# Sums of squares by a rounded square and its rest: two single-pass matmuls in place of one in fp32

## The chip, the cores and the metric

The kernel runs on one core of a Trainium2 chip. The metric is the device time of one execution in microseconds (us). The engines are TensorE (PE in the profile; its weight loads are listed as PEld), VectorE (DVE), ScalarE (ACT), GpSimd (POOL) and SyncE (SP), which here only issues the loads of weights.

## What is computed

One step of a one-layer encoder for 256 prompt tokens, 16 meta tokens and 32 sample tokens. The normalised input is multiplied by `w_in`. From the product come an attention branch with 16 heads and an mLSTM branch with 4 heads, and their gated outputs are multiplied by `w_out`. The change touches three RMS norms of the attention branch: that of the query latent (1536 columns), that of the queries (per head 128 columns and a rotary part of 64), and that of the keys (per head 128 columns):

```python
def rmsnorm(x, g):
    xf = x.astype(jnp.float32)
    y = xf * lax.rsqrt(jnp.mean(xf * xf, axis=-1, keepdims=True) + EPS)
    return (y * g.astype(jnp.float32)).astype(x.dtype)

q = (rmsnorm(cq_raw, q_a_norm) @ w_q_up).reshape(B, T, MLA_HEADS, QK_NOPE + QK_ROPE)
q_nope = rmsnorm(q[..., :QK_NOPE], q_nope_norm)
q_pe = rope(rmsnorm(q[..., QK_NOPE:], q_rope_norm), pos)
kv = (ckv @ w_kv_up).reshape(B, S, MLA_HEADS, QK_NOPE + V_HEAD)
k_nope = rmsnorm(kv[..., :QK_NOPE], k_nope_norm)
s = einsum(q_nope, k_nope) + einsum(q_pe, k_pe); p = softmax(s * ATTN_SCALE); attn = einsum(p, v)
```

## The kernel before

Features lie on the 128 partitions and tokens along the free dimension: 288 queries, 432 keys. Every large product is made of *units*. A unit is a 128-row slice of a weight matrix in `raw`. ScalarE casts it to fp32r, a rounded 32-bit form that TensorE takes in one pass (`whi`, line 490), VectorE subtracts the cast from the original (`wlo`, line 857), and TensorE does three fp32r matmuls for each 128 columns (`mm3`, lines 1297, 1300, 1301). ScalarE and VectorE work three units ahead of TensorE (`AHEAD`), and can start on unit k+3 when TensorE is done with unit k-1, because there are four slots.

Each engine runs a program written out by hand in a fixed order. The function `steps` does the split of unit k+3 and then calls `hooks(k)`, in which the small work of a stage is put. So what an engine does in hook k is behind the split of unit k+3 and ahead of the split of unit k+4, and a wait in a hook holds back every later split. On TensorE the hook of unit k comes behind the matmuls of unit k.

Stages that matter here:

- **ckv group** (32 units of 512 columns, 12 matmuls each). After units 2 to 13 `cq_squares` sums the squares of the query latent over the partitions by a matmul with a matrix of ones, in fp32 (line 1363). GpSimd makes the squares (line 1800) into `sqb`, which has three slots.
- **Eight head pairs.** A pair has 12 units for the queries (`q_units`, 9 matmuls each) and 4 for keys and values (`kv_units`, 18 matmuls each). Pair n+1 is projected while the attention of pair n is done in the hooks: `k_squares` at hook 1 (line 1499), `scores` of the two heads at hooks 5 and 8 (line 1510), `transposes` at 9 and 12, `weighted` at 11 and 13, and `q_squares` for the next pair at hook 14 (line 1457; at hook 13 in the first pair). The attention of the last pair runs in the hooks of the first mLSTM group, whose units have 12 matmuls.
- **At the end of a pair**, VectorE copies the raw keys out of PSUM (`k_evict`, line 994), then makes two products for the rotary part (lines 985, 986) and scales the two query heads in place (line 989). GpSimd squares the keys (line 1830), adds the rotary products (line 1835) and scales them for two heads (line 1840, `qpm`). ScalarE makes the inverse roots of the queries (`q_rstd`, lines 581 and 583, at hook 15) and then copies the values out (`v_evict`, line 611), which frees PSUM banks 1 and 2 for the next pair's queries.
- **Early in the next pair**, ScalarE makes the inverse roots of the keys at hook 1 (`k_rstd`). It waits there until the queries are scaled (`q_fin`) and the rotary part is scaled (`qp_fin`), because the roots of keys and queries share one buffer, `rsb`. VectorE scales the keys at hooks 2 and 3 (`k_norm`, line 1013). `scores` of the first head waits for the first of them.

```python
def k_rstd(phase, i, j):
    for t in range(2):
        b = 6 + t
        if t == 0:
            act.wait_ge(q_fin, 2 * j + 2)
            act.wait_ge(qp_fin, 2 * j + 2)
        rstd(rs2[:, t, :], bank[b][:, 0:NKV], 1.0 / NOPE, b, use(phase, b, 0, i), k_rs)
```

Of the kernel before, what the change touches and what calls it, by code (L numbers as in the profile page):

```python
# [28 lines left out]
P = 128  # L29
# [138 lines left out]
def hymba_step(nc, x_prompt, x_sample, cache_ckv, cache_kpe, state_C, state_n, state_m, meta, norm_gain,  # L168
# [8 lines left out]
    with ctx:  # L177
# [13 lines left out]
        nraw = sb("nraw", [72, NT])  # L191
        epsc = sb("epsc", [P, 1])
        gate_b = sb("gate_b", [ML_HEADS, 3])
        attnT = sb("attnT", [P, MLA_HEADS, NQ])

        def c(name, rows=P):
            a, w = CONST_AT[name]
# [30 lines left out]
        qpm = [sb2(f"qpm{h}", [P, SEQ + WIDE]) for h in range(2)]  # L228
        kn = sb2("kn", [P, 2, NKX])
        vt = sb2("vt", [P, 4, 2 * V_HEAD])  # L230
        sqb = sb2("sqb", [P, 3 * NQ])
        rsb = sb2("rsb", [P, 3 * NQ])
        rope1 = sb2("rope1", [P, NT])
        rope2 = sb2("rope2", [P, NT])
        rotq = sb2("rotq", [P, P])
# [5 lines left out]
        prob = keep(pa)("prob", [P, PROB_COLS])  # L241
        probT = keep(pa)("probT", [P, 608])
        pa.close()
        ckvf = sb2("ckvf", [P, KC, NT])
        p2.close()
        cqraw = attnT
        sq3 = sqb[:, :].rearrange("p (t n) -> p t n", t=3)
        sq2 = sqb[:, :].rearrange("p (t n) -> p t n", t=2)
        rs3 = rsb[:, :].rearrange("p (t n) -> p t n", t=3)
# [86 lines left out]
        gsc_d = sem("scaled_gains")  # L336
# [136 lines left out]
        def _(act):  # L473
# [76 lines left out]

            def ckv_hooks(k):

                if k == 16:
                    act.wait_ge(full[4], use("ckv", 4) + 1)
                    nc.scalar.activation(rs3[:, 0, :], bank[4][:, 0:NQ], ACT.Ln, scale=1.0 / Q_LORA,
                                         bias=epsc[:, :]).then_inc(free[4], 1)
                    act.wait_ge(free[4], use("ckv", 4) + 1)
                    nc.scalar.activation(rs3[:, 0, :], rs3[:, 0, :], ACT.Exp, scale=-0.5).then_inc(cq_rs, 1)
                if 18 <= k < 18 + KQ:
                    t = k - 18  # L560
                    act.wait_ge(cq_n, t + 1)
                    nc.scalar.copy(cqhi[:, t, :], cqraw[:, t, :]).then_inc(cq_hi, 1)
# [36 lines left out]
            def q_rstd(phase, i, n):  # L599

                for t in range(3):
# [2 lines left out]
                    rstd(rs3[:, t, :], bank[b][:, 0:NQ], 1.0 / (NOPE if t < 2 else ROPE), b,  # L604
                         use(phase, b, nth, i), q_rs)

            def v_evict(phase, i, n):
# [6 lines left out]
            def latent(k):  # L614
                if k == 7:
# [12 lines left out]
            q_rstd("bulk0", 0, 0)  # L628
            act.wait_ge(ck_out, 32)
            act.wait_ge(ck_tail_out, 32)  # L630
            v_evict("bulk0", 0, 0)
# [30 lines left out]

            def attention(phase, i, j):
                def hooks(k):
                    if k == 1:
                        k_rstd(phase, i, j)
                    if k == 6:
                        exps(phase, i, j, 0)
                    if k == 10:
                        pt_main(phase, i, j, 0)  # L670
                        exps(phase, i, j, 1)
                    if k == 12:
                        attn_evict(phase, i, j, 0)
# [10 lines left out]
            act.wait_ge(prob_zero, 1)  # L684
            for j in range(0, 6):
                steps(PAIR_UNITS, pair_units(j + 1), pair_units(j + 2), attention("step", j, j))
                v_evict("step", j, j + 1)
            steps(PAIR_UNITS, pair_units(7), big_units(U_ML, T_ML, 0, 2), attention("step", 6, 6))
            v_evict("step", 6, 7)


# [157 lines left out]
        def _(dve):  # L849
# [53 lines left out]
            ts_(rope1[:, 0:P], rot, G[:, G_KR:G_KR + 1], None, ALU.mult).then_inc(gsc_d, 1)  # L903

            def ckv_hooks(k):
                if 17 <= k < 17 + KQ + 1:
# [72 lines left out]
            def q_norm(phase, i, n):  # L979

                nth = 0 if phase == "bulk0" else 3
                if phase == "bulk0":
                    dve.wait_ge(kp_out, 64)
                dve.wait_ge(full[7], use(phase, 7, nth, i) + 1)
                tt(rope2[:, 0:NQ], bank[7][:, 0:NQ], sinT[:, N_META:NT], ALU.mult).then_inc(free[7], 1)
                stt(rope1[:, 0:NQ], qp[:, :], gsc[:, 1:2], cosT[:, N_META:NT], ALU.mult, ALU.mult).then_inc(qp_c, 1)
                for t in range(2):
                    dve.wait_ge(q_rs, 3 * n + t + 1)
                    stt(qn[:, t, :], qn[:, t, :], gsc[:, 0:1], rs3[:, t, :], ALU.mult, ALU.mult).then_inc(q_fin, 1)
# [5 lines left out]

            def first_pair(k):
                latent(k)
                if k == KQ - 1:
                    q_evict("bulk0", 0, 0)
                    dve.wait_ge(full[6], use("latent", 6, 2) + 1)  # L1000
# [3 lines left out]
            for t in range(2):  # L1004
                k_evict("bulk0", 0, 0, t)
            q_norm("bulk0", 0, 0)

            def k_norm(j, t):
                dve.wait_ge(k_rs, 2 * j + t + 1)
# [26 lines left out]

            def attention(phase, i, j):
                def hooks(k):
                    if k in (2, 3):
                        k_norm(j, k - 2)  # L1040
                    if k == 5:
                        maxima(phase, i, j, 0)
                    if k == 7:
# [6 lines left out]
                    if k == KQ - 1 and phase == "step":  # L1050
                        q_evict(phase, i, j + 1)
                    if k == 12:
                        pt_minor(phase, i, j, 1)
                return hooks

            def pair_end(i, n):
                for t in range(2):
                    k_evict("step", i, n, t)
                q_norm("step", i, n)

            def big_units(u):
                return lambda k: unit(u + k, k)
# [229 lines left out]
        def _(pe):  # L1292
# [64 lines left out]
            def cq_squares(k):  # L1357
                if 2 <= k < 2 + KQ:
                    t = k - 2
                    if t == 0:  # L1360
                        fill("ckv", 4)
                    pe.wait_ge(cq_sq, t + 1)
# [87 lines left out]
            def q_squares(phase, i, n):  # L1450

                first = phase == "bulk0"
                for t in range(3):
                    b = 4 + t
                    pe.wait_ge(q_sq, 3 * n + t + 1)
# [38 lines left out]
            def k_squares(phase, i, j):  # L1494
                for t in range(2):
                    b = 6 + t
                    pe.wait_ge(k_sq, 2 * j + t + 1)
# [488 lines left out]
```

## Time and profile before

| | |
|---|---|
| median of 3 runs | 2138.77 us (2137.19 to 2139.71) |
| the profiled execution | 2138.62 us |
| its span in the profile | 2137.0 us |
| mean granted TensorE clock | 0.997 |
| busy share: PE, DVE, ACT, POOL | 98%, 49%, 42%, 10% |

The profile is one execution. The span is the time from its first to its last instruction; 1.6 us of the execution lie around it. A share of busy time is a mean over stages. Lines such as L1499 are lines of the kernel before. A matmul with fp32 operands leaves two records for one instruction, and the records of matmuls overlap: what one costs is read from start to start, not from its duration. Starts and durations in a timeline are in us.

### The profile page before, as it was taken

How to read it: one execution, taken by the hardware profiler on the slowest of the kernel's cores; microseconds unless marked ns; L12 is line 12 of the kernel's file. 1: busy time of each engine (PE TensorE's matmuls, PEld its weight loads, DVE VectorE, ACT ScalarE, POOL GpSimd, SP SyncE). 2: the span in 40 equal slices, each digit the busy share in tenths (PEclk: the TensorE clock that was granted, in tenths of full speed). 3: DMA queues.
4: the chain of work that ended last, by engine and by line, in shares of the span. 5: the costliest groups of instructions: out<-in, count | busy, mean ns of one | idle time of the engine just before them, and what ended most of it. 6: DMA issues, size and time to landing. Idle time of an engine off the chain costs nothing.

```text
span 2137.0 us, 38018 instructions
## 1 busy us (share of the span) xinstructions
PE 2089.4 (98%) x15062; PEld 2029.1 (95%) x15062; DVE 1047.2 (49%) x1868; ACT 891.4 (42%) x1751; POOL 218.5 (10%) x292
## 2 busy tenths in 40 slices
PE   4999999999999999999999999999999999999997
PEld 3999999999999899998999999999999999999997
DVE  4544565655544444443444444444445654444443
ACT  4543454545443333343333444444444543333332
POOL 1000123333200000000000000000001100000000
PEclk9999999999999999999999999999999999999999
DMA  7555433232455454554545555555555555555553
GB/s 195 155 164 159 117 121 94 89 104 80 119 149 163 119 163 122 153 145 118 178 123 155 167 167 164 165 167 167 165 163 166 164 181 183 180 180 183 186 188 105
DMA packets 189984, 321.92 MB, mean 151 GB/s; under 512 B 20524, under 2 KB 65680, under 8 KB 189424
## 3 DMA queue, kind: packets, MB, share of 16 engines
q1 hardware_dynamic: 182464, 296.92, 47.0%
q0 software_dynamic: 5488, 15.11, 2.1%
q10 hardware_dynamic: 1872, 7.60, 1.4%
q8 instruction: 119, 1.95, 0.4%
q14 instruction: 41, 0.34, 0.1%
HBM read 309.96 MB, written 9.62 MB: 150 GB/s over the span
## 4 chain that ended last, share of the span: by engine, by line
PE 97%; DMA 1%; DVE 0%; ACT 0%; issue 0%; ACTq 0%; POOL 0%; POOLq 0%; DVEq 0%; SPq 0%
PE bank L1297 29%; PE bank L1301 28%; PE bank L1300 28%; DMA xt<-in_x_prompt_dram 1%; PE bank L1693 1%; PE bank L1656 1%; PE bank L1545 1%; PE bank L1442 1%; PE bank L1443 1%; PE bank L1440 1%; PE bank L1457 1%; PE bank L1499 1%; PE bank L1510 1%; PE bank L1511 1%; PE bank L1745 0%; PE bank L1323 0%
## 5 line engine op out<-in xcount | busy, mean ns | idle before, releaser
L857 DVE TENSOR_TENSOR wlo<-raw,whi 128x512 fp32r<-128x512 f32 (+1 forms) x1256 | 824.3, 665 | 987.3 <-ACT whi L490 984.1
L490 ACT CAST whi<-raw 128x512 fp32r<-128x512 f32 (+1 forms) x1256 | 713.0, 577 | 1085.4 <-PE bank L1301 1043.9
L1297 PE MATMUL bank<-xhi,whi 128*128 128x288 f32 (+2 forms) x3104 | 936.7, 302 | 1.5 <-DVE wlo L857 1.2
L1301 PE MATMUL bank<-xhi,wlo 128*128 128x288 f32 (+2 forms) x3104 | 925.3, 298 | 0.0
L1300 PE MATMUL bank<-xlo,whi 128*128 128x288 f32 (+2 forms) x3104 | 924.2, 298 | 0.0
L1297 PEld LDWEIGHTS bank<-xhi,whi 128*128 128x128 f32 (+1 forms) x3104 | 585.0, 188 | 5.2 <-DVE wlo L857 1.5
L1300 PEld LDWEIGHTS bank<-xlo,whi 128*128 128x128 f32 (+1 forms) x3104 | 585.4, 189 | 1.9 <-issue 1.1
L1301 PEld LDWEIGHTS bank<-xhi,wlo 128*128 128x128 f32 (+1 forms) x3104 | 584.1, 188 | 0.0
L1297 PE MATMUL bank<-mhi,whi 128*128 128x288 f32 x1024 | 304.0, 297 | 0.0
L1300 PE MATMUL bank<-mlo,whi 128*128 128x288 f32 x1024 | 302.5, 295 | 0.0
L1301 PE MATMUL bank<-mhi,wlo 128*128 128x288 f32 x1024 | 302.5, 295 | 0.0
L1297 PEld LDWEIGHTS bank<-mhi,whi 128*128 128x128 f32 x1024 | 193.2, 189 | 0.9
L1300 PEld LDWEIGHTS bank<-mlo,whi 128*128 128x128 f32 x1024 | 193.1, 189 | 0.0
L1301 PEld LDWEIGHTS bank<-mhi,wlo 128*128 128x128 f32 x1024 | 192.7, 188 | 0.0
L1297 PE MATMUL bank<-cqhi,whi 128*128 128x288 f32 x288 | 92.1, 320 | 1.3 <-ACT vt L611 0.7
L1301 PE MATMUL bank<-cqhi,wlo 128*128 128x288 f32 x288 | 85.0, 295 | 0.0
L1300 PE MATMUL bank<-cqlo,whi 128*128 128x288 f32 x288 | 84.8, 295 | 0.0
L1297 PEld LDWEIGHTS bank<-cqhi,whi 128*128 128x128 f32 x288 | 54.4, 189 | 5.2 <-DVE wlo L857 1.1
L1300 PEld LDWEIGHTS bank<-cqlo,whi 128*128 128x128 f32 x288 | 54.6, 189 | 1.3 <-issue 1.2
L1301 PEld LDWEIGHTS bank<-cqhi,wlo 128*128 128x128 f32 x288 | 54.4, 189 | 0.0
L1943 POOL DMA_DIRECT2D out_dram<-ytok x24 | 12.9, 540 | 391.2 <-DVE ytok L1270 388.4
L1850 POOL TENSOR_SCALAR prob<-prob,pinv 128x144 f32<-128x144 f32 (+2 forms) x48 | 40.7, 862 | 116.6 <-DVE pinv L1028 116.6
(314 smaller groups left out, 1377.5 us busy)
## 6 DMA issues: line engine op xcount, KB each, us to landing
raw<-in_w_in_dram SPq DMA_DIRECT2D x316, 512.0 KB, 3.8
raw<-in_w_out_dram SPq DMA_DIRECT2D x128, 512.0 KB, 3.7
raw<-in_w_in_dram SPq DMA_DIRECT2D x140, 256.0 KB, 2.9
raw<-in_w_q_up_dram SPq DMA_DIRECT2D x48, 384.0 KB, 3.3
raw<-in_w_kv_up_dram SPq DMA_DIRECT2D x16, 512.0 KB, 3.7
xres<-in_x_prompt_dram POOLq DMA_DIRECT2D x16, 256.0 KB, 4.9
out_dram<-ytok POOLq DMA_DIRECT2D x16, 256.0 KB, 3.1
C<-in_state_C_dram POOLq DMA_DIRECT2D x4, 512.0 KB, 5.1
```

What stands on the lines that cost most here:

```text
L490: ins = nc.scalar.copy(hi, src)
L857: ins = tt(lo, src, hi.bitcast(f32), ALU.subtract)
L1297: ins = mm(out, w_hi, m_hi, start=start, stop=False, **kw)
L1300: mm(out, w_hi, m_lo, start=False, stop=False, **kw)
L1301: return mm(out, w_lo, m_hi, start=False, stop=stop, **kw)
L1440: mm(out, ckhi[:, k, cs], vcols(whi), start=k == 0 and half == 0, stop=False, skip_group_check=True)
L1442: mm(out, cklo[:, k, cs], vcols(whi), start=False, stop=False, skip_group_check=True)
L1443: ins = mm(out, ckhi[:, k, cs], vcols(wlo), start=False, stop=last, skip_group_check=True)
L1457: mm(bank[b][:, 0:NQ], ones if t < 2 else blockones, sq3[:, t, :], start=True, stop=True)\
L1499: mm(bank[b][:, 0:NKV], ones, sq2[:, t, :], start=True, stop=True).then_inc(full[b], 1)
L1510: mm(out, qn[:, h, q0:q0 + P], kn[:, h, 0:keys], start=True, stop=False)
L1850: ts_(prob[0:n, at:at + w], prob[0:n, at:at + w], pinv[0:n, t:t + 1], None, ALU.mult).then_inc(pn, 1)
```

## The change

The squares are still made by GpSimd. ScalarE now makes a second square of the same input, rounded to fp32r (`cqsh`, `qsh`, `ksh`). VectorE subtracts it from GpSimd's square and writes the rest, in fp32r, over that square (`cqsl`, `qsl`, `ksl`). TensorE sums the two by two fp32r matmuls with `ones_r`, where it did one in fp32 with `ones`. The summing of the squares of the key/value latent and of the rotary key stays as it is. With it the order changes: the scaling of the queries moves from the end of the pair to VectorE's hook 1 of the next (`q_scale`), `k_squares` and `k_rstd` move from hook 1 to hook 2, and `k_norm` from hooks 2 and 3 to hooks 3 and 4. ScalarE's squares of the keys stand ahead of `v_evict`.

```diff
+        pt = ExitStack()
+        keep(pt)("attnT_", [P, MLA_HEADS - 2, NQ])
+        ksh0 = keep(pt)("ksh0", [P, 2 * NQ], f32r)
+        pt.close()
         attnT = sb("attnT", [P, MLA_HEADS, NQ])
+        ones_r = sb("ones_r", [P, P], f32r)
+        blockones_r = sb("blockones_r", [P, P], f32r)
...
-        sqb = sb2("sqb", [P, 3 * NQ])
-        rsb = sb2("rsb", [P, 3 * NQ])
+        ps = ExitStack()
+        sqb = keep(ps)("sqb", [P, 3 * NQ])
+        rsb = keep(ps)("rsb", [P, 3 * NQ])
+        ps.close()
+        sqr = sb2("sqr", [P, 3 * NQ], f32r)
+        rsr = sb2("rsr", [P, 3 * NQ], f32r)
...
+        cqsh = ksh0[:, :].rearrange("p (t n) -> p t n", t=2)
+        cqsl = sqr[:, :].rearrange("p (t n) -> p t n", t=3)
+        qsh, qsl = rsr[:, :].rearrange("p (t n) -> p t n", t=3), cqsl
+        ksh = (ksh0[:, 0:NKV], ksh1[:, :])
+        ksl = sqr[:, :].rearrange("p (t n) -> p t n", t=2)
```

On ScalarE in the ckv group:

```diff
+                if 1 <= k < 1 + KQ:
+                    t = k - 1
+                    act.wait_ge(free[1], use("ckv", 1))
+                    act.wait_ge(free[3], use("ckv", 3))
+                    if t >= 2:
+                        act.wait_ge(cq_ssm, t - 1)
+                    nc.scalar.activation(cqsh[:, t % 2, :], cqraw[:, t, :], ACT.Square).then_inc(cq_sqh, 1)
```

On ScalarE in the pairs (`q_square_hi` is called at hook 12 ahead of `attn_evict`, `k_square_hi` at the end ahead of `v_evict`):

```diff
+            def q_square_hi(phase, i, n):
...
+                for t in range(3):
+                    act.wait_ge(free[t], use(phase, t, 0, i) + 1)
+                    src = qn[:, t, :] if t < 2 else qp[:, :]
+                    nc.scalar.activation(qsh[:, t, :], src, ACT.Square).then_inc(q_sqh, 1)
+            def k_square_hi(phase, i, n):
+                for t, b in ((0, 3), (1, 0)):
+                    act.wait_ge(free[b], use(phase, b, (0, 1)[t], i) + 1)
+                    nc.scalar.activation(ksh[t], kn[:, t, 0:NKV], ACT.Square).then_inc(k_sqh, 1)
...
-                    if k == 1:
+                    if k == 2:
                         k_rstd(phase, i, j)
```

On VectorE (`cq_square_lo`, of the same kind, at hooks 1 to 12 of ckv, `q_square_lo` at hook 12 ahead of `pt_minor`, `k_square_lo` at the end of the pair):

```diff
+            nc.vector.tensor_copy(ones_r[:, :], ones).then_inc(ones_d, 1)
+            nc.vector.tensor_copy(blockones_r[:, :], blockones).then_inc(ones_d, 1)
...
+            def k_square_lo(n):
+                for t in range(2):
+                    dve.wait_ge(k_sq, 2 * n + t + 1)
+                    dve.wait_ge(k_sqh, 2 * n + t + 1)
+                    tt(ksl[:, t, :], sq2[:, t, :], ksh[t].bitcast(f32), ALU.subtract).then_inc(k_sql, 1)
+            def q_scale(n):
                 for t in range(2):
                     dve.wait_ge(q_rs, 3 * n + t + 1)
                     stt(qn[:, t, :], qn[:, t, :], gsc[:, 0:1], rs3[:, t, :], ALU.mult, ALU.mult).then_inc(q_fin, 1)
...
-                    if k in (2, 3):
-                        k_norm(j, k - 2)
+                    if k == 1:
+                        q_scale(j)
+                    if k in (3, 4):
+                        k_norm(j, k - 3)
```

On TensorE:

```diff
-                    ins = mm(bank[4][:, 0:NQ], ones, sq3[:, t % 3, :], start=t == 0, stop=t == KQ - 1)
+                    mm(bank[4][:, 0:NQ], ones_r[:, :], cqsh[:, t % 2, :], start=t == 0, stop=False)
+                    ins = mm(bank[4][:, 0:NQ], ones_r[:, :], cqsl[:, t % 3, :], start=False, stop=t == KQ - 1)
...
-                    mm(bank[b][:, 0:NQ], ones if t < 2 else blockones, sq3[:, t, :], start=True, stop=True)\
-                        .then_inc(full[b], 1)
+                    w = (ones_r if t < 2 else blockones_r)[:, :]
+                    mm(bank[b][:, 0:NQ], w, qsh[:, t, :], start=True, stop=False)
+                    mm(bank[b][:, 0:NQ], w, qsl[:, t, :], start=False, stop=True).then_inc(full[b], 1)
...
-                    mm(bank[b][:, 0:NKV], ones, sq2[:, t, :], start=True, stop=True).then_inc(full[b], 1)
+                    mm(bank[b][:, 0:NKV], ones_r[:, :], ksh[t], start=True, stop=False)
+                    mm(bank[b][:, 0:NKV], ones_r[:, :], ksl[:, t, :], start=False, stop=True).then_inc(full[b], 1)
...
-                    if k == 1:
+                    if k == 2:
                         k_squares(phase, i, j)
```

## Rows read from the trace of the kernel before

**Rows 1.** The page: busy time, share of the span and instructions of each engine

```profile
PE 2089.4 (98%) x15062; PEld 2029.1 (95%) x15062; DVE 1047.2 (49%) x1868; ACT 891.4 (42%) x1751; POOL 218.5 (10%) x292
```

**Rows 2.** Groups by line and form, TensorE: records, busy us, mean ns

```profile
L1457 PE MATMUL bank<-sqb,con 128*128 128x288 f32 x48 | 12.9, 406 | 0.0
L1499 PE MATMUL bank<-sqb,con 128*128 128x432 f32 x32 | 12.9, 525 | 0.0
...
L1363 PE MATMUL bank<-sqb,con 128*128 128x288 f32 x24 | 7.8, 405 | 0.0
```

**Rows 3.** Timeline of TensorE, end of pair 1 and start of 2: start, us

```profile
339.00 1.62 PE L1457 MATMUL bank<-sqb,con 128*128 128x288 f32 x6
...
341.14 0.36 PE L1300 MATMUL bank<-cklo,whi 128*128 128x432 f32 x1
341.33 0.35 PE L1301 MATMUL bank<-ckhi,wlo 128*128 128x432 f32 x1
...
346.06 1.61 PE L1499 MATMUL bank<-sqb,con 128*128 128x432 f32 x4
...
347.64 0.29 PE L1300 MATMUL bank<-cqlo,whi 128*128 128x288 f32 x1
...
348.97 0.29 PE L1301 MATMUL bank<-cqhi,wlo 128*128 128x288 f32 x1
...
352.46 0.41 PE L1510 MATMUL bank<-kn,qn 128*128 128x144 f32 x2
```

**Rows 4.** Timeline of ScalarE in the same stretch

```profile
342.02 0.45 ACT L583 ACTIVATE rsb<-rsb 128x288 f32<-128x288 f32 x1
343.02 1.30 ACT L611 COPY vt<-bank 128x512 f32<-128x512 f32 x2 [0.56 <-PE bank L1443]
...
347.62 0.62 ACT L581 ACTIVATE rsb<-bank,epsc 128x432 f32<-128x432 f32 x1 [1.88 <-POOL qpm L1840]
348.27 0.57 ACT L583 ACTIVATE rsb<-rsb 128x432 f32<-128x432 f32 x1
```

**Rows 5.** Timeline of VectorE and GpSimd there, in windows of single instructions

```profile
342.65 0.91 POOL L1830 TENSOR_TENSOR sqb<-kn 128x432 f32<-128x432 f32 x1 [10.34 <-DVE kn L994]
343.20 0.66 DVE L986 SCALAR_TENSOR_TENSOR rope<-qp,gsc,con 128x288 f32<-128x288 f32 x1
343.51 1.12 POOL L1830 TENSOR_TENSOR sqb<-kn 128x432 f32<-128x432 f32 x1
343.79 1.16 DVE L989 SCALAR_TENSOR_TENSOR qn<-qn,gsc,rsb 128x288 f32<-128x288 f32 x1
344.60 1.01 POOL L1835 TENSOR_TENSOR rope<-rope 128x288 f32<-128x288 f32 x1
344.87 1.06 DVE L989 SCALAR_TENSOR_TENSOR qn<-qn,gsc,rsb 128x288 f32<-128x288 f32 x1
345.79 0.81 POOL L1840 TENSOR_TENSOR qpm<-rope,rsb 64x288 f32<-64x288 f32 x1 [0.18 <-POOL rope L1835]
345.85 1.03 DVE L857 TENSOR_TENSOR wlo<-raw,whi 128x256 fp32r<-128x256 f32 x1
346.68 0.86 POOL L1840 TENSOR_TENSOR qpm<-rope,rsb 64x288 f32<-64x288 f32 x1
```

**Rows 6.** Timeline of VectorE alone, later in that stretch

```profile
345.85 2.37 DVE L857 TENSOR_TENSOR wlo<-raw,whi 128x256 fp32r<-128x256 f32 x4
...
351.29 0.67 DVE L1013 SCALAR_TENSOR_TENSOR kn<-kn,G,rsb 128x432 f32<-128x432 f32 x1
```

**Rows 7.** Timeline, first pair's keys: ScalarE's root, TensorE's scores

```profile
310.63 0.62 ACT L581 ACTIVATE rsb<-bank,epsc 128x432 f32<-128x432 f32 x1 [1.34 <-PE bank L1499]
315.84 0.41 PE L1510 MATMUL bank<-kn,qn 128*128 128x144 f32 x2
```

**Rows 8.** The same two for the last pair, in the mLSTM group

```profile
567.72 0.62 ACT L581 ACTIVATE rsb<-bank,epsc 128x432 f32<-128x432 f32 x1 [1.77 <-PE bank L1499]
574.71 0.41 PE L1510 MATMUL bank<-kn,qn 128*128 128x144 f32 x2
```

More of the change, by code:

```diff
@@ L243, in hymba_step @@
         pa.close()
+        pb = ExitStack()
+        keep(pb)("prob_", [P, PROB_COLS])
+        ksh1 = keep(pb)("ksh1", [P, NKV], f32r)
+        pb.close()
         ckvf = sb2("ckvf", [P, KC, NT])
@@ L335, in hymba_step @@
             "kpe_stored", "rope_zeroed", "qn_zeroed", "barred_in", "kpe_rows", "ckv_out", "ckv_tail_out", "kpe_out"))
-        gsc_d = sem("scaled_gains")
+        gsc_d, ones_d = sem("scaled_gains"), sem("ones_rounded")
+        cq_sqh, cq_sql, q_sqh, q_sql, k_sqh, k_sql = (sem(n) for n in (
+            "cq_square_hi", "cq_square_lo", "q_square_hi", "q_square_lo", "k_square_hi", "k_square_lo"))
         q_sq, q_rs, q_fin = (sem(n) for n in ("q_squares", "q_rstd", "q_normed"))
@@ L605, in q_rstd @@
                          use(phase, b, nth, i), q_rs)
+            def q_square_hi(phase, i, n):
+                if n == 0:
+                    act.wait_ge(ck_n, KC)
+                    act.wait_ge(kp_n, 1)
+                else:
+                    act.wait_ge(k_fin, 4 * n)
+                for t in range(3):
[6 more added lines that the diff above has]
+                    nc.scalar.activation(ksh[t], kn[:, t, 0:NKV], ACT.Square).then_inc(k_sqh, 1)
             def v_evict(phase, i, n):
@@ L614, in latent @@
             def latent(k):
+                if k == 12:
+                    q_square_hi("bulk0", 0, 0)
                 if k == 7:
@@ L628, in _ @@
             q_rstd("bulk0", 0, 0)
+            k_square_hi("bulk0", 0, 0)
             act.wait_ge(ck_out, 32)
@@ L672, in hooks @@
                     if k == 12:
+                        if phase == "step":
+                            q_square_hi(phase, i, j + 1)
                         attn_evict(phase, i, j, 0)
@@ L686, in _ @@
                 steps(PAIR_UNITS, pair_units(j + 1), pair_units(j + 2), attention("step", j, j))
+                k_square_hi("step", j, j + 1)
                 v_evict("step", j, j + 1)
             steps(PAIR_UNITS, pair_units(7), big_units(U_ML, T_ML, 0, 2), attention("step", 6, 6))
+            k_square_hi("step", 6, 7)
             v_evict("step", 6, 7)
@@ L901, in _, with cq_square_lo @@
             ts_(rotq[:, :], rot, gsc[:, 1:2], None, ALU.mult).then_inc(gsc_d, 1)
+            nc.vector.tensor_copy(ones_r[:, :], ones).then_inc(ones_d, 1)
+            nc.vector.tensor_copy(blockones_r[:, :], blockones).then_inc(ones_d, 1)
             nc.vector.memset(qn_[:, 2 * NQ:SEQ + NQ + WIDE], 0.0).then_inc(qn_zero, 1)
             ts_(rope1[:, 0:P], rot, G[:, G_KR:G_KR + 1], None, ALU.mult).then_inc(gsc_d, 1)
+            def cq_square_lo(t):
+                dve.wait_ge(cq_sq, t + 1)
+                dve.wait_ge(cq_sqh, t + 1)
+                tt(cqsl[:, t % 3, :], sq3[:, t % 3, :], cqsh[:, t % 2, :].bitcast(f32), ALU.subtract).then_inc(cq_sql, 1)
             def ckv_hooks(k):
+                if 1 <= k < 1 + KQ:
+                    cq_square_lo(k - 1)
                 if 17 <= k < 17 + KQ + 1:
@@ L986, in q_norm, with q_square_lo @@
                 stt(rope1[:, 0:NQ], qp[:, :], gsc[:, 1:2], cosT[:, N_META:NT], ALU.mult, ALU.mult).then_inc(qp_c, 1)
+            def q_square_lo(n):
+                for t in range(3):
+                    dve.wait_ge(q_sq, 3 * n + t + 1)
+                    dve.wait_ge(q_sqh, 3 * n + t + 1)
+                    tt(qsl[:, t, :], sq3[:, t, :], qsh[:, t, :].bitcast(f32), ALU.subtract).then_inc(q_sql, 1)
+            def k_square_lo(n):
[4 more added lines that the diff above has]
+            def q_scale(n):
                 for t in range(2):
@@ L997, in first_pair @@
                 latent(k)
+                if k == KQ:
+                    q_square_lo(0)
                 if k == KQ - 1:
@@ L1006, in _ @@
             q_norm("bulk0", 0, 0)
+            k_square_lo(0)
             def k_norm(j, t):
@@ L1052, in hooks @@
                     if k == 12:
+                        if phase == "step":
+                            q_square_lo(j + 1)
                         pt_minor(phase, i, j, 1)
@@ L1059, in pair_end @@
                 q_norm("step", i, n)
+                k_square_lo(n)
             def big_units(u):
@@ L1361, in cq_squares @@
                         fill("ckv", 4)
-                    pe.wait_ge(cq_sq, t + 1)
-                    ins = mm(bank[4][:, 0:NQ], ones, sq3[:, t % 3, :], start=t == 0, stop=t == KQ - 1)
+                        pe.wait_ge(ones_d, 2)
+                    pe.wait_ge(cq_sql, t + 1)
+                    mm(bank[4][:, 0:NQ], ones_r[:, :], cqsh[:, t % 2, :], start=t == 0, stop=False)
+                    ins = mm(bank[4][:, 0:NQ], ones_r[:, :], cqsl[:, t % 3, :], start=False, stop=t == KQ - 1)
                     ins.then_inc(full[4] if t == KQ - 1 else cq_ssm, 1)
@@ L1454, in q_squares @@
                     b = 4 + t
-                    pe.wait_ge(q_sq, 3 * n + t + 1)
+                    pe.wait_ge(q_sql, 3 * n + t + 1)
                     fill(phase, b, 0 if first else (2, 4, 3)[t], i)
-                    mm(bank[b][:, 0:NQ], ones if t < 2 else blockones, sq3[:, t, :], start=True, stop=True)\
-                        .then_inc(full[b], 1)
+                    w = (ones_r if t < 2 else blockones_r)[:, :]
+                    mm(bank[b][:, 0:NQ], w, qsh[:, t, :], start=True, stop=False)
+                    mm(bank[b][:, 0:NQ], w, qsl[:, t, :], start=False, stop=True).then_inc(full[b], 1)
                 pe.wait_ge(gsc_d, 3)
@@ L1496, in k_squares @@
                     b = 6 + t
-                    pe.wait_ge(k_sq, 2 * j + t + 1)
+                    pe.wait_ge(k_sql, 2 * j + t + 1)
                     fill(phase, b, 0, i)
-                    mm(bank[b][:, 0:NKV], ones, sq2[:, t, :], start=True, stop=True).then_inc(full[b], 1)
+                    mm(bank[b][:, 0:NKV], ones_r[:, :], ksh[t], start=True, stop=False)
+                    mm(bank[b][:, 0:NKV], ones_r[:, :], ksl[:, t, :], start=False, stop=True).then_inc(full[b], 1)
             def scores(phase, i, j, h):
```

## Prediction

> **What bounds the kernel now.** I read the page's busy times first [rows 1]: TensorE is at work 98% of the span, so an instruction taken from it shortens the kernel, unless the engine then waits. Next I read the groups by form, for what the change can take away [rows 2]. The reader is to see the counts: 24, 48 and 32 records, two to an fp32 instruction, so 12 sums for the query latent, 24 for the queries (8 pairs of 3) and 16 for the keys (8 pairs of 2). Last I read the timelines of a pair's end on all engines [rows 3 to 6], because the change puts work on three engines between that end and the next pair's first scores. Here the reader is to look at who is late for whom. ScalarE's key root starts at 347.62 after 1.88 us of idling, released by GpSimd [rows 4]. The first head's keys are scaled at 351.29 + 0.67 = 351.96 [rows 6], and TensorE begins the scores at 352.46 [rows 3]. That is a spare of only 0.5 us. TensorE is busy there, but the side chain is almost as long as its work.
>
> **What TensorE saves.** From 339.00 to 341.14 lie four fp32 matmuls of 288 columns (three sums and the rotation, which stays) and one fp32r matmul of 432 [rows 3]. The latter steps by 341.33 - 341.14 = 0.19, so one fp32 matmul of 288 costs (2.14 - 0.19) / 4 = 0.487. Fp32r matmuls of 288 take ten steps from 347.64 to 348.97, 0.133 each. For the keys, 346.06 to 347.64 less one step is 1.45 for two, 0.725 each, against 2 x 0.195 in fp32r. That fp32r keeps its step with a matrix of ones as weights is assumed: the weights are of the same shape and size as in the rows.
> - Query latent: 12 x (0.487 - 0.266) = 2.7 us.
> - Queries: per pair 3 x 0.22 = 0.66 us, in 8 pairs 5.3.
> - Keys: per pair 1.45 - 0.78 = 0.67 us, in 8 pairs 5.4.
>
> Together 13.3 us, if TensorE never waits for it. Below nothing can't be, since the matmuls are fewer passes; above 13.3 there is nothing on TensorE to save.
>
> **Query latent.** Per unit of TensorE (12 matmuls, 1.6 us) this adds a square on ScalarE (0.45, as the 288-column exponential [rows 4]) and a subtraction on VectorE (at most the 1.16 of a two-operand instruction that meets GpSimd [rows 5]). They lie beside TensorE's matmuls: each engine has one split per unit besides, and TensorE asks for the rest a whole unit after the hook in which it is made. Without that cover each would cost its own length. The two copies of ones stand ahead of a split that TensorE wants three units later, so they cost nothing. I take the full 2.7 us.
>
> **Queries at hook 12.** Three squares on ScalarE (3 x 0.45 at most) stand ahead of `attn_evict` and of the copy of transposed probabilities for `weighted` at hook 13; three subtractions on VectorE (0.3 to 1.1 each) ahead of its own copy for the same. Both copies wait for `transposes` at hook 12, and then TensorE has a unit of 18 matmuls, some 2.4 us, before it wants them. I cost both at nothing; without this cover they would put up to 1.5 us a pair before `weighted`.
>
> **The end of a pair, values.** ScalarE's last root of the queries ends at 342.02 + 0.45 = 342.47 [rows 4], and what follows can overlap it by the 0.07 that two VectorE instructions do (343.86 and 343.79 [rows 5]). The values' copy now stands behind two squares of 432 (0.57 each at 348.27, so 0.50 from start to start). It starts at 343.40 and not at 343.02, while TensorE wants bank 1 0.66 earlier. TensorE's first unit of the next pair is thus over at about the old time: the 0.66 of the queries is gone by here, and some 0.1 more.
>
> **The end of a pair, the port.** The rows of VectorE and GpSimd [rows 5] show more. Whenever VectorE has two operands in SBUF while GpSimd works, each ends a fixed time after the other: GpSimd at 343.56, VectorE at 343.86; then 344.63 and 344.95; 345.61 and 345.93; 346.60 and 346.88; and GpSimd's last at 347.54. They take turns. A turn of VectorE is 0.30 to 0.32 for 288 columns and 0.28 for 256, I take 0.48 for 432; a turn of GpSimd is 0.77 for 432 columns and 0.66 for its 288s. The new order puts two subtractions of 432 into these turns and the scaling of the queries behind two splits. With the pair's end 0.66 earlier:
> - GpSimd's first key square ends at 343.56 - 0.66 = 342.90, VectorE's rotary product at 343.21, GpSimd's second square at 343.98, the first subtraction at 344.46 (ScalarE's squares, due 342.97 and 343.47, are no hindrance).
> - GpSimd's sum to 345.12, second subtraction to 345.60, `qpm` to 346.27, first part of the split of unit 3 to 346.55, `qpm` to 347.21.
> - The rest of units 3 and 4 takes what it takes now, from 347.54 to 345.85 + 2.37 = 348.22 [rows 6], so to 347.89.
> - Now `q_scale`, two of 288 without an opponent: about 0.5 each (between a turn, 0.32, and the 0.67 of a free 432 [rows 6]), less 0.07 of overlap. It ends at 348.8.
>
> The key root waits for `q_fin`, as `rsb` is shared. It starts at 348.9 and not at 347.62. TensorE's own sums, now at hook 2, would allow 347.9. From the root's start to the scaled key it takes 351.96 - 347.62 = 4.34 now and the same after, since one split follows the roots in either order. The scores then start at 348.9 + 4.34 + 0.1 = 353.3, against 352.46: 0.84 us later, where TensorE alone would have been there at about 351.8. Queued behind the root on ScalarE are the splits of units 6 on, behind `k_norm` on VectorE the split of unit 7 and the maxima; they follow the later scores in step. Both savings of such a pair (1.33 us) are gone and 0.84 us come on top. Bounds for one pair: -0.1 us, if the turns cost no more than free instructions and the root is held only by TensorE's sums; +1.9 us, if a subtraction in turns takes 1.16 x 432 / 288 = 1.74 and not some 1.2. I take the turns, since all nine rows fit them.
>
> On this the Trainium skill, "SBUF — State Buffer", section "SBUF: two separate sides", says that VectorE with two SBUF inputs and GpSimd take one port pair as an exclusive lock for a whole instruction. The trace agrees (1.16 for what leaves 0.32 after GpSimd's end). By the rule the pair costs +0.84; by a shared bandwidth, with no blocking, it would be near -0.1.
>
> **First and last pair.** In the first, the root starts at 310.63, held by TensorE, and the scores at 315.84 [rows 7], 0.7 us after their keys (310.63 + 4.34 = 314.97). The same turns from a later start bring the root to some 311.7 and the scores to 316.2: +0.4 us. In the last, the following units are of 12 matmuls (1.6 us) and the root is held by TensorE's sums: from 567.72 it moves a unit, less 0.35 for its faster first sum, to 569.0, the keys are ready at 573.4, and TensorE comes at 574.71 - 0.6 = 574.1 [rows 8]. One saving stays, -0.6 us.
>
> **The sum.** -2.7 (latent) + 0.4 (first) + 6 x 0.84 (pairs in between, 5.0) - 0.6 (last) = +2.1 us on the profiled execution's 2138.62 us, which is 0.15 us below the median of the runs. That is 2140.8 us, slower by 0.1%. About 0.2% (4.3 us) is what a measurement of this kernel can tell from no change, so the forecast counts as the same.
>
> **Rivals.**
> - *All of it arrives.* TensorE is 98% busy and its idle time before these sums is 0.0 [rows 1, 2], so 13.3 us less: 2125.3. Against it: the spare of 0.5 us ahead of the scores, and a root that waits already. In part: a pair that kept half of its 1.33 us would give -2.7 - 0.6 - 6 x 0.67 = -7.3, 2131. Together 0.13.
> - *No turns.* VectorE's subtractions cost 0.6 and are done before GpSimd's `qpm`; the root waits for TensorE's sums alone. Then -2.7 + 0.2 - 6 x 0.1 - 0.6 = -3.7, 2135: the same, just. For it: the 432-column product at 351.29 takes 0.67 with GpSimd idle. Against it: rows 5. Chance 0.14.
> - *Slower.* The chain from the subtractions to `q_scale` is longer than I have it, because GpSimd gets in two more turns of 0.66 ahead of VectorE: the root at 350.2, the scores at 354.6, 2.1 us a pair, and the sum -2.9 + 12.9 = +10, 2148.8. For it: every VectorE instruction with two inputs there ends behind one of GpSimd. It decides from 1.2 us a pair, 0.36 more than I take, so it needs little. Chance 0.25.
> - My forecast, with its own range 2137 to 2143: 0.48.
>
> So faster by over 0.2% has 0.13, slower by over 0.2% 0.27 (the third rival and an edge of mine), the same 0.60. The range: 2134 leaves out the first rival, 2148 most of the third's far side.
>
> **What the profile after would show.** Right: the fp32r sums step by 0.13 and 0.19; TensorE idles or stretches ahead of the first scores of each middle pair (1.5 us), its waits put down to the scaled keys; the key root's idle is released by VectorE's L989 and no longer by GpSimd; the time from one middle pair's scores to the next's longer by about 0.8 us; a ckv group shorter by 2.7. Wrong: the key root released by TensorE's sums (no turns), that time shorter than now (the saving arrives), a subtraction over 1.3 us or `weighted` waiting at hook 13 (slower). I would also be wrong if fp32r with ones stepped slower than 0.13, or if ScalarE's squares cost more than its exponentials.

## The result and the profile after

| | before | after |
|---|---|---|
| median of 13 runs each | 2140.62 us | 2145.07 us |
| lowest and highest | 2137.19 to 2143.03 | 2143.09 to 2147.22 |
| the profiled execution | 2138.62 us | 2144.49 us |
| its span | 2137.0 us | 2142.9 us |

The ratio of after to before is 1.0023, with a 95% interval of 1.0015 to 1.0030: the change costs some 4.9 us, where 2.1 were forecast. It comes out at the edge of what I had called measurable (0.2%), on the slower side of it. By the medians the difference is 4.5 us. The 13 runs of before also show that the three of the table ahead lay at the low end: the median of after lies within the forecast's wide range (2134 to 2148) and beyond the narrower one that I had given my own theory (2137 to 2143). Both stood on an execution of 2138.62 us, 2.0 below the median of before here.

First the page of the kernel after: busy time of each engine, and the shares of the chain that ended last.

```profile
PE 2080.8 (97%) x15062; PEld 2027.4 (95%) x15062; DVE 1074.6 (50%) x1922; ACT 909.5 (42%) x1803; POOL 222.4 (10%) x292
...
PE 93%; DVE 3%; ACT 2%; DMA 1%; issue 1%; ACTq 0%; POOL 0%; POOLq 0%; DVEq 0%; SPq 0%
```

TensorE is busy 8.6 us less than in [rows 1] and the span is 5.9 us longer. (The 8.6 isn't the saving itself: records overlap, and this execution has one more stretch at the lower clock, shown below.) The chain, which lay on TensorE for 97% of the span before, now leaves it for VectorE and ScalarE. What TensorE waits for is in the view of its waits, kernel after (us in total, times, longest):

```profile
PE bank L1601 <- DVE kn L1095: 10.3, 7, 1.6
PE bank L1384 <- ACT vt L657: 4.8, 8, 1.6
```

Before, there was no wait for `kn` at the scores, and a single one for `vt`, of 0.7 us. Both are per pair. The next fences are a middle pair of the kernel after. It is a pair later than [rows 3 to 6]: its query sums start at 374.64 where those of [rows 3] start at 339.00, so 35.64 is taken off to compare. TensorE:

```profile
374.64 0.29 PE L1547 MATMUL bank<-rsr,ones_r 128*128 128x288 f32 x1
374.77 0.30 PE L1548 MATMUL bank<-sqr,ones_r 128*128 128x288 f32 x1
...
378.78 0.29 PE L1388 MATMUL bank<-cqhi,wlo 128*128 128x288 f32 x1
379.53 0.40 PE L1384 MATMUL bank<-cqhi,whi 128*128 128x288 f32 x1 [0.46 <-ACT vt L657]
379.77 0.29 PE L1387 MATMUL bank<-cqlo,whi 128*128 128x288 f32 x1
379.90 0.29 PE L1388 MATMUL bank<-cqhi,wlo 128*128 128x288 f32 x1
380.04 0.38 PE L1384 MATMUL bank<-cqhi,whi 128*128 128x288 f32 x1
380.26 0.29 PE L1387 MATMUL bank<-cqlo,whi 128*128 128x288 f32 x1
...
382.91 0.36 PE L1589 MATMUL bank<-ksh,ones_r 128*128 128x432 f32 x1
383.11 0.36 PE L1590 MATMUL bank<-sqr,ones_r 128*128 128x432 f32 x1
...
387.14 0.29 PE L1388 MATMUL bank<-cqhi,wlo 128*128 128x288 f32 x1
389.02 0.48 PE L1601 MATMUL bank<-kn,qn 128*128 128x144 f32 x2 [1.59 <-DVE kn L1095]
```

The matmuls got cheaper as assumed: steps of 0.13 for 288 columns and 0.20 for 432. ScalarE, VectorE and GpSimd in the same stretch, the latter two in windows of single instructions:

```profile
378.01 1.01 ACT L651 ACTIVATE ksh<-kn 128x432 fp32r<-128x432 f32 x2
378.92 1.04 ACT L657 COPY vt<-bank 128x512 f32<-128x512 f32 x2
...
384.43 0.62 ACT L609 ACTIVATE rsb<-bank,epsc 128x432 f32<-128x432 f32 x1 [1.91 <-DVE qn L1068]
```

```profile
378.50 1.12 POOL L1921 TENSOR_TENSOR sqb<-kn 128x432 f32<-128x432 f32 x1
378.78 1.31 DVE L1062 TENSOR_TENSOR sqr<-sqb,ksh 128x432 fp32r<-128x432 f32 x1
379.58 1.17 POOL L1926 TENSOR_TENSOR rope<-rope 128x288 f32<-128x288 f32 x1
...
380.93 0.96 POOL L1931 TENSOR_TENSOR qpm<-rope,rsb 64x288 f32<-64x288 f32 x1 [0.18 <-POOL rope L1926]
381.14 1.04 DVE L910 TENSOR_TENSOR wlo<-raw,whi 128x256 fp32r<-128x256 f32 x1
381.97 0.88 POOL L1931 TENSOR_TENSOR qpm<-rope,rsb 64x288 f32<-64x288 f32 x1
```

```profile
378.78 2.44 DVE L1062 TENSOR_TENSOR sqr<-sqb,ksh 128x432 fp32r<-128x432 f32 x2
381.14 2.39 DVE L910 TENSOR_TENSOR wlo<-raw,whi 128x256 fp32r<-128x256 f32 x4
383.46 0.94 DVE L1068 SCALAR_TENSOR_TENSOR qn<-qn,gsc,rsb 128x288 f32<-128x288 f32 x2
...
388.09 0.67 DVE L1095 SCALAR_TENSOR_TENSOR kn<-kn,G,rsb 128x432 f32<-128x432 f32 x1
```

Each VectorE instruction again ends just behind one of GpSimd. In the last of the three views, the queries' scaling ends at 384.40; the key root starts 0.03 later. TensorE's two matmuls for the first key head had started at 382.91 and 383.11: they don't decide when the root starts. From there the chain to the scores takes 389.02 - 384.43 = 4.59 us, against 4.84 before, 0.5 of which was spare.

TensorE's account of the pair, from start to start. It saves 1.33 us. The step to the matmul behind the wait for `vt` is 0.75 (from 378.78) instead of 0.13, and two of the next steps are 0.24 and 0.22: 0.82 lost. The step to the scores is 1.88 (from 387.14), so 1.75 lost. Before, the same stretch had lost 0.34 in four longer steps, at 344.37 and 351.16, which no wait in the profile names. That is 1.33 - 0.82 - 1.75 + 0.34 = -0.90, and the scores are at 389.02 - 35.64 = 353.38 against 352.46, 0.92 later. The idle times in brackets (0.46 and 1.59) are shorter than the steps because they count from the modelled end of the matmul before.

### The profile page after: what moved, and what is told of

Its sections match the earlier page's. It is cut to its first block, busy times and chain, and to the rows that moved or that the text cites. A ratio compares the mean times of both kernels' runs of the same rounds, so it can differ in the third digit from the quotient of the medians.

```text
span 2142.9 us, 38196 instructions
## 1 busy us (share of the span) xinstructions
PE 2080.8 (97%) x15062; PEld 2027.4 (95%) x15062; DVE 1074.6 (50%) x1922; ACT 909.5 (42%) x1803; POOL 222.4 (10%) x292
## 4 chain that ended last, share of the span: by engine, by line
PE 93%; DVE 3%; ACT 2%; DMA 1%; issue 1%; ACTq 0%; POOL 0%; POOLq 0%; DVEq 0%; SPq 0%
PE bank L1384 28%; PE bank L1387 27%; PE bank L1388 27%; DVE wlo L910 1%; DMA xt<-in_x_prompt_dram 1%; PE bank L1784 1%; PE bank L1747 1%; PE bank L1636 1%; PE bank L1601 1%; ACT rsb L609 1%; PE bank L1532 1%; PE bank L1531 1%; PE bank L1529 1%; PE bank L1602 1%; ACT whi L511 0%
```

## The experiments

In each, the time from one middle pair's first scores to the next's in the trace is called the period: 36.63 us before (36.61 to 36.67), 37.62 after. Medians of before, on whose runs the ratios rest, were 2140.7 to 2141.1. A difference of medians can lie up to 1.1 us from what the ratio gives. Places in a trace can be compared between kernels only from the first sum for the latent on: this sum starts at 202.80 us before and at 202.68 to 204.87 in the other profiles, though no matmul ahead of it was changed.

**The query latent alone.** Queries and keys are as before; 24 fp32 records of TensorE become 24 fp32r matmuls.

```diff
-                    ins = mm(bank[4][:, 0:NQ], ones, sq3[:, t % 3, :], start=t == 0, stop=t == KQ - 1)
+                    mm(bank[4][:, 0:NQ], ones_r[:, :], cqsh[:, t % 2, :], start=t == 0, stop=False)
```

> Only the sums for the query latent are changed; queries and keys are as in the kernel before. Both theories: the ckv group is 2.7 us shorter and nothing after it takes this back, so -2.7 us against the kernel before (ratio 0.9988). If the saving were taken back at the first head pair it would be 0.

Measured: 2138.89 us, 0.9991 (0.9982 to 1.0000), so -1.9 us, with 2.7 inside the interval and 0 at its edge; period 36.6 as before. In the trace of the change itself the latent's sums follow each other by 1.945 us instead of 2.16, so 11 steps save 2.4. In this kernel's own trace the stretch from the first of these sums to the first sum for the queries takes 93.70 us, against 96.07 before: 2.4 less as well. From the first of them to the last scores it is also 2.4 less, so the pairs don't take it back. (Without that starting point the saving can't be seen, since the first sum itself starts 2.07 us later in this profile.)

**Latent and queries, keys as before.** The key sums, the place of `q_scale`, `k_squares` and `k_norm` are those of before.

```diff
-            k_square_lo(0)
+            q_scale(0)
...
-                    mm(bank[b][:, 0:NKV], ones_r[:, :], ksh[t], start=True, stop=False)
-                    mm(bank[b][:, 0:NKV], ones_r[:, :], ksl[:, t, :], start=False, stop=True).then_inc(full[b], 1)
+                    mm(bank[b][:, 0:NKV], ones, sq2[:, t, :], start=True, stop=True).then_inc(full[b], 1)
```

> Latent and queries changed, the whole part of the keys (squares, subtractions, hooks 1 to 3) as before. My theory (the loss comes from the keys' subtractions and the queries' scaling behind them): the queries keep their 0.66 us in each of 8 pairs, so -2.6 - 5.3 = -7.9 us against before (ratio 0.9963), and TensorE has no wait for scaled keys. Rival (the three squares and subtractions at hook 12, or any hastening of the pair's end, are what costs): no better than the latent alone, -2.7 us.

Measured: 2129.04 us, 0.9949 (0.9935 to 0.9962). The period is 35.97, so 0.66 less than before: all of what the query sums save arrives. The last scores start 7.3 us earlier (567.45, against 574.71 in [rows 8]), or 7.7 counted from the first sum for the latent, where 7.9 was expected. The ratio gives 10.9 us; the rest of it lies behind the pairs, as told below under what no term held. The keys' part of the change therefore costs 37.62 - 35.97 = 1.65 us a pair.

**A memory of their own for the key roots.** The roots go into two tiles that are idle then (the last two heads' part of `attnT`, and `probT`; not the rounded squares that the expectation names), and the waits for the scaled queries move to the next writer of `rsb`. All else is as after.

```diff
-                    if t == 0:
-                        act.wait_ge(q_fin, 2 * j + 2)
-                        act.wait_ge(qp_fin, 2 * j + 2)
-                    rstd(rs2[:, t, :], bank[b][:, 0:NKV], 1.0 / NOPE, b, use(phase, b, 0, i), k_rs)
+                    rstd(rk[t], bank[b][:, 0:NKV], 1.0 / NOPE, b, use(phase, b, 0, i), k_rs)
```

> As after, but the key roots are written over the used-up rounded squares of the keys and not into the queries' root buffer, so they no longer wait for the scaled queries. My theory: the root starts with TensorE's sums, some 0.9 us earlier in each middle pair, and the scores come as much earlier: 6 x 0.9 = 5.4 us less than after, about 1 us less than before. Rival (VectorE's own backlog holds the scaled key, whoever waits for the queries): as after.

Measured: 2138.31 us, 0.9988 (0.9978 to 0.9997), 6.8 us less than after. Waits of TensorE, this kernel:

```profile
PE bank L1384 <- ACT vt L660: 4.8, 8, 1.6
PE bank L1601 <- DVE kn L1095: 4.6, 7, 0.7
```

The period is 36.70, 0.9 less than after, and the root is released by TensorE's own sum (L1590) though the subtractions and the scaling take as long as in after (2.43 and 0.94 us for two of each). The wait for `vt` has not changed. So the reuse of `rsb` is what makes the longer VectorE queue count.

**The scaling of the queries back at the pair's end**, ahead of the two subtractions:

```diff
+                q_scale(n)
                 k_square_lo(n)
...
-                    if k == 1:
-                        q_scale(j)
```

> As after, but VectorE scales the queries at the end of the pair, ahead of the keys' two subtractions. My theory: by turns of the two engines the subtractions end 2 us later (TensorE waits 0.3 us for them at hook 2), but the root no longer waits for the queries and starts 0.5 us earlier: 6 x 0.5 = 3 us less than after. Rival (the place of the scaling doesn't matter, only the amount of VectorE's work): as after.

Measured: 2138.67 us, 0.9989 (0.9980 to 0.9998), 6.4 us less than after; period 36.79. The queries are now scaled in turns with GpSimd, 1110 ns each instead of 507, and yet the chain is shorter, since the subtractions no longer stand ahead of what the root waits for. The scaling ends at 381.05, long before TensorE's sums at 383.05, and the root is released by L1590. I had expected 3 us and a wait of 0.3 for the subtractions: they end at 383.33, the second is wanted only by TensorE's last sum at 383.68, and TensorE has no idle time there.

**GpSimd's share shortened.**

```diff
-                tt(rope1[:, 0:NQ], rope1[:, 0:NQ], rope2[:, 0:NQ], ALU.add).then_inc(qp_a, 1)
+                tt(rope1[:, 0:16], rope1[:, 0:16], rope2[:, 0:16], ALU.add).then_inc(qp_a, 1)
...
-                    tt(qpm[h][s, 0:NQ], rope1[s, 0:NQ], rs3[s, 2, :], ALU.mult).then_inc(qp_fin, 1)
+                    tt(qpm[h][s, 0:16], rope1[s, 0:16], rs3[s, 2, 0:16], ALU.mult).then_inc(qp_fin, 1)
```

> As after, but GpSimd's sum and its two products for the rotary queries are cut to 16 of 288 columns (so most of the rotary queries are left out). Theory of turns: VectorE's instructions beside them no longer wait for GpSimd: the second subtraction falls from 1.2 us to 0.6, the two splits behind from 2.4 to 1.2, the key root is then held by TensorE's sums alone, and each middle pair is 0.9 us shorter, 5 to 6 us less than after. Rival (VectorE's instructions are long by themselves, or for another reason): durations as in after, and the time as well.

Measured: 2138.67 us, 0.9987 (0.9977 to 0.9996), 6.4 us less than after; period 36.80. VectorE's work is the same in both kernels; this one leaves out most of the rotary queries. The two subtractions of a middle pair in windows of single instructions, of after and of this kernel:

```profile
378.78 1.31 DVE L1062 TENSOR_TENSOR sqr<-sqb,ksh 128x432 fp32r<-128x432 f32 x1
380.01 1.21 DVE L1062 TENSOR_TENSOR sqr<-sqb,ksh 128x432 fp32r<-128x432 f32 x1
```

```profile
379.54 1.31 DVE L1062 TENSOR_TENSOR sqr<-sqb,ksh 128x432 fp32r<-128x432 f32 x1
380.77 0.62 DVE L1062 TENSOR_TENSOR sqr<-sqb,ksh 128x432 fp32r<-128x432 f32 x1
```

ScalarE's roots of the keys, groups by form from 310 to 560 us (count, busy us, mean ns, idle time before), of the same two:

```profile
L609 ACT ACTIVATE rsb<-bank,epsc 128x432 f32<-128x432 f32 x13 | 8.0, 612 | 11.4 <-DVE qn L1068 11.4
```

```profile
L609 ACT ACTIVATE rsb<-bank,epsc 128x432 f32<-128x432 f32 x14 | 8.6, 613 | 7.5 <-PE bank L1590 7.5
```

The first subtraction still runs beside GpSimd's full second square and takes 1.31 us in both kernels. The second runs beside the shortened sum and falls from 1.21 to 0.62, as expected, and with it and the splits behind it the root is no longer late. This is what the rival without turns had denied. The Trainium skill, "SBUF — State Buffer", section "SBUF: two separate sides", has GpSimd and a VectorE instruction with two SBUF inputs holding one port pair for a whole instruction each; the 0.59 us that the second subtraction gains from GpSimd's having less to do agrees with it.

**Values ahead of the squares.** ScalarE copies the values first and squares the keys after it. The rival theory was that the copy of the values, standing behind the squares, takes the saving.

```diff
-                k_square_hi("step", j, j + 1)
                 v_evict("step", j, j + 1)
+                k_square_hi("step", j, j + 1)
```

> As after, but ScalarE copies the values out ahead of the squares of the keys. Rival theory (the values' copy behind the squares is a cost of its own: TensorE waits 4.8 us for it in the profile): 4 us less than after. My theory: TensorE only arrives earlier at a wait that is set elsewhere; the wait for the values goes, the wait for the scaled keys grows by as much, and the time is that of after within 1 us.

Measured: 2146.98 us, 1.0025 (1.0016 to 1.0035). Waits of TensorE:

```profile
PE bank L1601 <- DVE kn L1095: 14.7, 7, 2.1
...
PE bank L1384 <- ACT vt L657: 0.7, 1, 0.7
```

The wait for `vt` is gone and the one for `kn` has grown by about as much: the subtractions wait for the later squares (1.00 us of VectorE's idle time ahead of them in a middle pair). I had expected the time of after within 1 us; it is 1.9 us longer by the medians. The periods are 0.15 longer, and part of the rest is a fall of the clock, told at the end. The copy of the values is not what sets the time of the change; it only takes back early what the keys' chain would take later.

**Key roots of their own, and the key steps at hooks 1, 2 and 3**, as before the change:

```diff
-                    if k == 2:
+                    if k == 1:
                         k_rstd(phase, i, j)
...
-                    if k in (3, 4):
-                        k_norm(j, k - 3)
+                    if k in (2, 3):
+                        k_norm(j, k - 2)
```

> As own_roots (key roots in a place of their own), with the keys' sums, roots and scaling back at hooks 1, 1 and 2, 3. My theory: the subtractions end at about the time of hook 1, so TensorE waits little for them, the root starts 0.7 us or more earlier, and no wait for scaled keys stays: some 0.7 us less per middle pair than own_roots, 4 to 5 us in all. Rival (hook 1 comes before the subtractions are done and TensorE stands there as long as it gains): as own_roots.

Measured: 2130.75 us, 0.9952 (0.9938 to 0.9965); period 35.81, no wait for `kn`, and still 4.9 us for `vt`. That is 7.6 us less than with roots of their own alone, by the medians, where 4 to 5 were expected; 6 x 0.89 = 5.3 of it is in the periods, and most of the rest goes with the clock (the table further down). Now that the side chain has time to spare, the wait for `vt` does count, as the next kernel shows.

**The same, and ScalarE's order mixed**: first half of the values, first key square, second half, second square.

```diff
                 for half, b in ((0, 1), (1, 2)):
+                    if half:
+                        k_square_hi(phase, i, n, 0)
...
+                k_square_hi(phase, i, n, 1)
```

> As own_hook1, with ScalarE's order at the end of the pair: values' first copy, square of key 0, values' second copy, square of key 1. My theory: with no chain longer than TensorE's work, the saving of the sums now arrives: middle pairs 1.2 us shorter than before, all together 11 to 12 us less than before (ratio 0.9945). Rival (the port's turns still hold VectorE's splits): no better than the variant with latent and queries alone.

Measured: 2127.94 us, 0.9936 (0.9923 to 0.9950), 13 us less than before. ScalarE at a pair's end, timeline of this kernel:

```profile
339.73 0.58 ACT L662 COPY vt<-bank 128x512 f32<-128x512 f32 x1
340.21 0.57 ACT L654 ACTIVATE ksh<-kn 128x432 fp32r<-128x432 f32 x1
340.68 0.57 ACT L662 COPY vt<-bank 128x512 f32<-128x512 f32 x1
341.14 0.57 ACT L654 ACTIVATE ksh<-kn 128x432 fp32r<-128x432 f32 x1
...
343.59 0.62 ACT L610 ACTIVATE attnT<-bank,epsc 128x432 f32<-128x432 f32 x1 [0.88 <-PE bank L1590]
```

The period is 35.37, 0.44 less, about the length of the wait for `vt` that is gone: 1.26 of the 1.33 us that TensorE saves in a pair arrive. The last scores start at 563.45, 11.3 us before those of [rows 8], or 11.9 counted from the first sum for the latent. So the change's arithmetic was worth nearly the 13.3 us forecast if nothing waits, and its order had spent them.

## Why the prediction was right, and what it missed

The mechanism was right step by step. The size was less so: +4.9 us (4.5 by the medians) for +2.1.

**TensorE's saving** (13.3 us if nothing waits): right. The steps are 0.13 and 0.20, ones as weights cost nothing extra, and the last kernel delivers 11.9 us of it in its trace.

**Query latent, -2.7:** right within what can be told (2.4 in 11 steps; -1.9 by itself, interval 0 to -3.9).

**Queries at hook 12, at nothing:** right; with only the queries changed the period falls by the whole 0.66.

**Values:** right. The 0.66 was to be gone by the end of the first unit of the next pair. The second unit starts at 380.52 - 35.64 = 344.88, and before it started at 344.88 too. The long step and the slower ones behind it take 0.82, of which before had 0.15.

**The turns:** right, and shown by shortening GpSimd's side. In the frame of [rows 3 to 6] the subtractions end at 344.45 and 345.58 (forecast 344.46 and 345.60), `q_scale` at 348.76 (348.8), the root starts at 348.79 (348.9), TensorE waits 1.59 (1.5), the scores start at 353.38 (353.3).

**The reason the root is late:** right. It is the wait for `q_fin` through `rsb`; either a root memory of its own or a shorter queue ahead of the scaling undoes 0.8 to 0.9 us a pair. The bound worked out for a root held only by TensorE, 0.1 us less than before, came out as 0.07 more (36.70).

**The sum** is where the size was off. First scores of the first pair, counted from the first sum for the latent: 111.11 us against 113.04, so -1.93, where -2.7 + 0.4 = -2.3 was forecast; it is -2.4 up to the sums for the queries and +0.5 behind them. (The prediction says that before TensorE came 0.7 us after the keys there; its own numbers, 315.84 and 314.97, give 0.87.) Last pair -0.57 (period 38.54 against 39.11), forecast -0.6. The mis-sized term is that of the pairs in between: 6 x 0.84 = 5.0 was 6 x 0.99 = 5.9. Of the 0.15, 0.08 is the chain's (0.92), and the rest lies outside it, between the scores and the next pair's end: 23.25 us against 23.16, the scores' first matmuls after the wait taking 0.48 instead of 0.41. By the last scores that makes -1.93 + 5.93 - 0.57 = +3.4 us (578.02 - 574.71 = +3.3 from the start of the spans), for a forecast of +2.1.

**What no term held.** The two profiled executions differ by 5.9 us, so 2.6 more lie behind the pairs, where the change touches nothing. The windows of 10 us from 600 us on in which the granted clock is clearly below 1 (columns: busy us of each engine, clock, DMA share, GB/s), before and after:

```profile
750.00:760.00 10.00, 10.00 (x63) 9.94 (x64) 4.51 (x10) 3.20 (x6) 0.79 (x1) 0.83 0.34 113
880.00:890.00 10.00, 9.92 (x62) 9.67 (x63) 4.25 (x9) 3.04 (x6) 0.75 (x1) 0.83 0.38 119
```

```profile
750.00:760.00 10.00, 10.00 (x58) 9.04 (x58) 3.27 (x5) 1.88 (x4) 0.00 (x0) 0.83 0.19 54
1010.00:1020.00 10.00, 10.00 (x58) 9.04 (x57) 3.05 (x5) 2.06 (x4) 0.00 (x0) 0.83 0.18 52
1140.00:1150.00 10.00, 10.00 (x60) 9.04 (x59) 3.50 (x7) 2.86 (x4) 0.29 (x1) 0.83 0.28 74
```

Each holds a piece in which TensorE has the lower of its two clocks (1.2 GHz), and loses 0.17 x 10 = 1.7 us. Before has two of them, after three: 1.7 of the 2.6 us. The kernel with latent and queries changed has none; its span of 2127.2 us is 9.8 below that of before, for 7.3 at the last scores.

Single profiles can't tell how often this happens, but each run on record also has its mean granted clock, to 0.001. The 47 runs of before that were made beside the experiments take, on average, 2142.3 us at 0.995, 2141.0 at 0.996, 2139.9 at 0.997 and 2138.4 at 0.998. The runs of after take 2145.8 at 0.995 (nine runs) and 2143.2 at 0.997 (three); the only one at 0.996 takes 2145.0, 4.0 more. So at the two clocks with more than one run the change costs 3.3 to 3.4 us, which is what its trace shows in the pairs. The rest goes with a lower mean clock, 0.9955 against 0.9960, which is worth 0.0005 x 2140 = 1.1 us. The same reckoning for all kernels, in us against before (the sum of trace and clock is an estimate, the last column is the difference of the mean times):

| kernel | last scores, counted from the first sum for the latent | mean clock of its runs | sum | measured |
|---|---|---|---|---|
| after | +3.4 | +1.1 | +4.5 | +4.6 |
| latent alone | -2.4 | +0.4 | -2.1 | -2.0 |
| latent and queries | -7.7 | -3.3 | -11.0 | -11.0 |
| own roots | -2.3 | +0.2 | -2.2 | -2.4 |
| scaling back | -1.5 | -1.0 | -2.5 | -2.1 |
| GpSimd shortened | -1.5 | -2.1 | -3.7 | -2.7 |
| values first | +7.4 | +0.9 | +8.3 | +5.7 |
| own roots, hooks 1 to 3 | -8.4 | -1.7 | -10.1 | -10.0 |
| the same, order mixed | -11.9 | -0.9 | -12.7 | -13.2 |

The kernel with the values first is off because its profile has two falls of the clock ahead of the last scores, 3.2 us together, which stand in both columns. For after, the last column would be +4.1 against the mean of the 47 runs. By this estimate some quarter of what after loses, and more than a quarter of what latent and queries gain, goes with the clock. Whether the changed order makes such pieces more frequent or after had bad luck in 13 runs is not shown; I had no term for it.

## What to carry to other kernels

An engine that is 98% busy still doesn't pass a saving on, if the side chain that feeds its next step has less to spare than the saving (0.5 us here, against 1.33): measure that spare before putting new work on the engines of the chain. Look for waits that protect a reused buffer (here the key roots behind the scaled queries), because work queued ahead of the buffer's last reader lengthens them; a buffer of its own, or the reader first, made 0.8 to 0.9 us a pair here, the buffer at no cost because two tiles were idle. When the profile shows two engines ending in turn, count their instructions as one queue.

## What the runs showed that I had not expected

**The clock after a wait.** In the kernel with the values first, TensorE waits 2.0 to 2.1 us ahead of the scores in each pair but the last. After two of these waits the granted clock falls. Windows of that kernel: the first begins just behind the start of such scores at 315.65, the second and third hold those at 355.03 and 392.82:

```profile
316.00:326.00 10.00, 10.00 (x59) 9.06 (x59) 5.69 (x19) 3.15 (x11) 2.42 (x3) 0.85 0.46 124
...
354.00:364.00 10.00, 8.97 (x60) 8.48 (x61) 7.26 (x23) 3.82 (x15) 2.43 (x3) 1.00 0.41 131
...
392.00:402.00 10.00, 9.18 (x50) 8.40 (x51) 5.70 (x20) 3.81 (x14) 2.37 (x3) 0.83 0.37 96
```

The periods that begin with a fall are 39.4 us, the others 37.8: 1.6 us each, nearly the wait over again. The waits of 1.6 us in the kernel after were not followed by one. Why a wait of the same length brings a fall at one pair and none at the next stays open.

**Where the clock falls behind the pairs.** The 13 runs of before went from 2137.2 to 2143.0 us. The profiles of all ten kernels together show 18 pieces at the lower clock behind the pairs, and they stand at four places only, one for each mLSTM head and some 130 us apart. At each place TensorE does eight fp32 matmuls of a single column, two records each (kernel before, the first of the four places):

```profile
748.92 1.40 PE L1706 MATMUL bank<-con,kws 128*128 128x1 f32 x12
750.18 0.58 PE L1709 MATMUL bank<-con,kws 72*128 72x1 f32 x4
```

Every one of the 18 pieces begins 1.4 to 2.6 us after the start of the first of these, here at 751.1, and lasts 3.4 us. The profile counts TensorE as busy for 98 to 100% of the 10 us around. The other 22 of the 40 places bring none, and what decides between the two stays open, as it does for the waits above. The profiles have none to three pieces of 1.7 us each, which is of a size to make most of the spread of the runs. That these matmuls bring the fall is argued from where it stands: a kernel without them there would test it, and none was run.
